# Conditioning matmuls from raw fp32 weights in four 32-column tiles, with buffers of their own for the head

## The chip, the core and the metric

The kernel runs on one core of one Trainium2 chip. The core has five engines: PE (TensorE, matmuls), DVE (VectorE), ACT (ScalarE), POOL (GpSimd) and SP (SyncE, which here only issues DMAs). The metric is the time of one execution on the device in microseconds (us).

## What is computed

A transformer-like model of two blocks, all in fp32, 256 tokens of `x` and 256 of `ctx`, width 1024. The first block has two layers; each is steered by nine conditioning vectors per stream, made from one vector `c` (for `x`) or `c_ctx` (for `ctx`). The change is about these vectors:

```python
mx = jnp.split(jax.nn.silu(c) @ ada_w[layer] + ada_b[layer], N_MOD, axis=-1)
mc = jnp.split((jax.nn.silu(c_ctx) @ ada_w[layer] + ada_b[layer])[None, :], N_MOD, axis=-1)
x = x + 0.5 * mx[2][:, None] * swiglu(modulate(rms_norm(x), mx[0], mx[1]), ffn1_w_gu[layer], ffn1_w_down[layer])
...
hx = modulate(rms_norm(x), mx[3], mx[4])
...
x = x + mx[5][:, None] * merge_mixers(...)
x = x + 0.5 * mx[8][:, None] * swiglu(modulate(rms_norm(x), mx[6], mx[7]), ffn2_w_gu[layer], ffn2_w_down[layer])
```

Here `modulate(h, shift, scale)` is `h * (1 + scale) + shift`. So 18 groups (two layers, nine vectors) are needed, each a product of two vectors of 1024 with a matrix of 1024x1024. The rest, feed-forward layers, a mixer of attention, pooling and a Fourier transform, and a second block with four other mixers, is not touched by the change except for the numbering of its weights.

## The kernel before

**Slots.** All weights come from one array `stream` of 816 slots of 128x1024 fp32 (512 KB each) in the order of use. SP loads slot n into `raw[n % 4]` (a ring of four). ACT makes the upper half, `whi` (fp32r, L1033); DVE the rest, `wlo = raw - whi` (L1491); both are rings of four too. PE waits for `w_ready` and multiplies in three fp32r matmuls (`mm3`, L419 to L421): upper times upper, upper times lower, lower times upper. A slot of `raw` is loaded again when its `wlo` is done (`w_ready`), a slot of `whi` and `wlo` is written again when PE is done with it (`slots_done`).

**The conditioning.** A group is eight slots (one for each 128 of the contraction). The vectors silu(c) and silu(c_ctx) are the stationary operand, as `cst4`: four columns (upper and lower of both), padded to 128. `ada` (L506 to L513) gives for each slot four fp32r matmuls with 512 columns into banks 4 and 5: two halves of the slot, each with `whi` and `wlo`. After eight slots ACT copies 4x1024 to `ada_row` (`ada_rows`, L1139), PE transposes it in eight pieces of 4x128 (`ada_cols`, L527), and DVE adds both parts and `ada_b` into `mod` (`ada_mod`, L1678 and L1681).

**Where the groups stand.** Two at the start (`ada_head`, 16 slots; before them nothing can be normalised, as `fix`, made from the scale of group 1, enters `norm_mod`). Five in `ffn1_up0`, five in `ffn2_up0`, four in `ffn1_up1`: there a loop handles 16 slots a pass, eight up-projection tiles (gate and up in turn, 24 matmuls with 512 columns each, the first two interleaved in `joint_tiles`) and eight conditioning slots between them, as `ADA_GROUP` says. Two more in `in0`, the first layer's mixer input: after each of tiles 1 to 8 two conditioning slots. So 14 groups are in loops, two in `in0`, two in the head.

**Order.** Everything is by hand: each engine has its own program, with waits on semaphores. In `ffn_up` ACT and DVE split the slots three or four ahead of PE and do a unit (silu of the gate, product with up, split into `hh` and `hl`) for each pair of tiles. In the head, ACT's squares of `X` for the first norm stand between the splits of slots 11 to 15, POOL adds them (L2094), PE sums (`norm_sums`, L438), ACT takes the root, PE spreads it; then DVE and ACT make `nh` and `nl` (`norm_mod`, L1566, and L1075, L1556), and the first `joint_tiles` follows them.

## Time and profile before

| | us |
|---|---|
| median of three runs | 3071.42 |
| lowest, highest | 3066.06, 3074.35 |
| span of the profiled execution | 3071.1 |
| PE busy | 2945.6 (96%) |
| DVE busy | 1690.4 (55%) |
| ACT busy | 1332.7 (43%) |
| POOL busy | 204.1 (7%) |

The profile shows one execution. An instruction's row has its start from the beginning of the span and its length; matmuls are pipelined, so their distance counts and not their length. A share of busy time is an average over stages: a loss is read from what an engine waited for in a stage. The granted clock is the share of TensorE's full clock (1.0 is 2.4 GHz, 0.5 is 1.2 GHz) that it was given.

### The profile page before, as it was taken

The numbers are of one execution on the slowest core, as the hardware profiler recorded it, in microseconds if no ns is written. First come the engines' busy times: TensorE is split into PE (matmuls) and PEld (weight loads), VectorE is DVE, ScalarE is ACT, GpSimd is POOL, SyncE is SP. The second block draws the span as 40 slices with busy tenths as digits, with TensorE's granted clock in tenths as the row PEclk, the third lists the DMA queues.
The fourth block names the chain that finished last, engine by engine and source line by source line (L and its number), as shares of the span: only waits on it lengthen the run. The fifth ranks groups of instructions, "written<-read, shape, count | busy, mean of one in ns | idle before, by whom it ended". The sixth has DMA issues, their size and how long they took to land. (4 is left out here: it accounts for less than half of the span.)

```text
span 3071.1 us, 48943 instructions
## 1 busy us (share of the span) xinstructions
PE 2945.6 (96%) x17866; PEld 2573.3 (84%) x17866; DVE 1690.4 (55%) x2279; ACT 1332.7 (43%) x1862; POOL 204.1 (7%) x224
## 2 busy tenths in 40 slices
PE   6999999999999999999988999899999999999998
PEld 5878887567787878888866998899999999998998
DVE  6444326646444244443265556976557476659864
ACT  5433325335343134332244445554545345545553
POOL 1000001200000000000020001300300000003100
PEclk7999999999999999999988999999999999999999
DMA  6445324113444225443222554355536556553453
GB/s 217 159 149 171 117 89 159 55 42 123 150 159 148 96 73 167 157 137 98 94 98 100 184 188 137 111 168 197 179 120 192 192 174 216 191 174 104 162 196 132
DMA packets 120488, 443.57 MB, mean 144 GB/s; under 512 B 13568, under 2 KB 14976, under 8 KB 119744
## 3 DMA queue, kind: packets, MB, share of 16 engines
q1 hardware_dynamic: 119376, 431.38, 42.6%
q0 software_dynamic: 1008, 10.75, 0.9%
q8 instruction: 71, 1.16, 0.2%
q14 instruction: 33, 0.27, 0.0%
HBM read 441.03 MB, written 1.05 MB: 144 GB/s over the span
## 5 line engine op out<-in xcount | busy, mean ns | idle before, releaser
L1491 DVE TENSOR_TENSOR wlo<-raw,whi 128x1024 fp32r<-128x1024 f32 x816 | 1001.0, 1240 | 922.4 <-ACT whi L1033 911.3
L1033 ACT ACTIVATE whi<-raw 128x1024 fp32r<-128x1024 f32 x816 | 848.8, 1054 | 942.7 <-PE ps L421 920.4
L419 PE MATMUL ps<-nh,whi 128*128 128x512 f32 (+1 forms) x1696 | 626.0, 369 | 20.1 <-DVE nl L1556 17.3
L420 PE MATMUL ps<-nl,whi 128*128 128x512 f32 (+1 forms) x1696 | 620.9, 366 | 0.0
L421 PE MATMUL ps<-nh,wlo 128*128 128x512 f32 (+1 forms) x1696 | 620.6, 366 | 0.0
L419 PE MATMUL ps<-bh,whi 128*128 128x256 f32 x1664 | 479.1, 288 | 10.8 <-DVE bl L1578 7.6
L420 PE MATMUL ps<-bl,whi 128*128 128x256 f32 x1664 | 468.8, 282 | 0.0
L421 PE MATMUL ps<-bh,wlo 128*128 128x256 f32 x1664 | 468.6, 282 | 0.0
L419 PEld LDWEIGHTS ps<-nh,whi 128*128 128x128 f32 x1696 | 323.0, 190 | 83.5 <-issue 19.3
L421 PEld LDWEIGHTS ps<-nh,wlo 128*128 128x128 f32 x1696 | 322.5, 190 | 56.1
L420 PEld LDWEIGHTS ps<-nl,whi 128*128 128x128 f32 x1696 | 323.0, 190 | 54.3 <-issue 0.2
L419 PEld LDWEIGHTS ps<-bh,whi 128*128 128x128 f32 x1664 | 314.8, 189 | 19.2 <-DVE bl L1578 13.0
L420 PEld LDWEIGHTS ps<-bl,whi 128*128 128x128 f32 x1664 | 315.1, 189 | 0.5
L421 PEld LDWEIGHTS ps<-bh,wlo 128*128 128x128 f32 x1664 | 315.0, 189 | 0.0
L419 PE MATMUL ps<-mh,whi 128*128 (+1 forms) x1024 | 287.7, 281 | 0.0
L420 PE MATMUL ps<-ml,whi 128*128 (+1 forms) x1024 | 287.7, 281 | 0.0
L421 PE MATMUL ps<-mh,wlo 128*128 (+1 forms) x1024 | 287.7, 281 | 0.0
L421 PE MATMUL ps<-hh,wlo 128*128 (+2 forms) x704 | 259.6, 369 | 0.0
L419 PE MATMUL ps<-hh,whi 128*128 (+2 forms) x704 | 257.9, 366 | 0.0
L420 PE MATMUL ps<-hl,whi 128*128 (+1 forms) x528 | 207.7, 393 | 0.0
L419 PEld LDWEIGHTS ps<-mh,whi 128*128 128x128 f32 x1024 | 192.9, 188 | 0.0
L420 PEld LDWEIGHTS ps<-ml,whi 128*128 128x128 f32 x1024 | 192.9, 188 | 0.0
(216 smaller groups left out, 3354.5 us busy)
## 6 DMA issues: line engine op xcount, KB each, us to landing
raw<-stream SPq DMA_DIRECT2D x816, 512.0 KB, 3.4
gates_w<-gate_in POOLq DMA_DIRECT2D x2, 3328.0 KB, 13.5
cst<-cst_in POOLq DMA_DIRECT2D x2, 1280.0 KB, 5.8
X<-x_in SPq DMA_DIRECT2D x1, 2048.0 KB, 11.7
out<-X SPq DMA_DIRECT2D x8, 128.0 KB, 2.0
fftw<-fftw_in POOLq DMA_DIRECT2D x2, 256.0 KB, 5.8
ws<-ws_in POOLq DMA_DIRECT2D x1, 512.0 KB, 4.4
poolw<-poolw_in POOLq DMA_DIRECT2D x2, 128.0 KB, 5.6
```

Of the source, the lines that this page charges most:

```text
L419: pe.matmul(dst, w1, rhs_hi, start=start, stop=False)
L420: pe.matmul(dst, w1, rhs_lo, start=False, stop=False)
L421: return pe.matmul(dst, w2, rhs_hi, start=False, stop=stop)
L1033: act.activation(whi[:, r, :], raw[:, r, :], ACT.Copy).then_inc(w_hi_ready, 1)
L1491: dve.tensor_tensor(wlo[:, r, :], raw[:, r, :], whi[:, r, :].bitcast(F32), ALU.subtract).then_inc(w_ready, 1)
```

## The change

Conditioning slots are not split any more. The two silu vectors lie in `csil`, fp32, padded to 32 columns. For a pair of slots PE issues four plain fp32 matmuls (`ada_streams`): each half of each slot goes to one quarter of bank 4's partitions, which is one 32-column tile of the array. One bank is used instead of two. ACT copies all 128 partitions of it (128x512) to `ada_row`; `ada_cols` multiplies four blocks of `ada_row` with `pick`, a 128x4 pattern of ones that adds even and odd slots; DVE adds `ada_b` in one instruction.

The slots are numbered anew: `AT` counts the split ones ("main") alone, `ORDER` is the order of loading, `SOURCE` the slot in `stream`, `PLACE` the place in the order. The ring `raw` still has four places, shared by both kinds: a place that held a main slot is free at its `w_ready`, one that held a conditioning slot at `ada_mm`, which PE raises after the pair. In a pass of the loop a pair stands behind tiles 2, 3, 4 and 5 (of 0 to 7).

The 16 slots of the head go to buffers of their own (`head`, in memory used later by the hidden layer), in eight DMAs of two slots; `X` is loaded first, and the squares are made at once. SP's loop is written out.

```diff
+ADA_AFTER = {2: 0, 3: 1, 4: 2, 5: 3}
...
+            def load(n):
+
+                if n >= RING:
+                    before, q = ORDER[n - RING]
+                    if before == "main":
+                        sp.wait_ge(w_ready, q + 1)
+                    else:
+                        sp.wait_ge(ada_mm, q // 2 + 1)
+                sp.dma_start(raw[:, n % RING, :], stream[SOURCE[n]]).then_inc(raw_loaded[n % RING], 16)
...
             sp.dma_start(cvec[:], cvec_in).then_inc(cond_loaded, 16)
...
             sp.dma_start(X[:], x_in).then_inc(x_loaded, 16)
...
+            for n in range(HEAD_PAIRS):
+                if n == 4:
+                    sp.dma_start(ident[:], ident_in).then_inc(vec_loaded, 16)
+                    sp.dma_start(ada_b[:], ada_b_in).then_inc(vec_loaded, 16)
+                    sp.dma_start(vec[:], vec_in).then_inc(vec_loaded, 16)
+                if n == HEAD_PAIRS - 1:
+                    load(0)
+                    load(1)
+                load_head(n)
+            for n in range(2, len(ORDER)):
+                load(n)
...
-            def ada(at, dyn, kt):
-
-                weights(at, dyn)
-                for b in range(2):
-                    for w in (whi, wlo):
-                        last = pe.matmul(bank(4 + b), cst4[:, 4 * kt:4 * kt + P],
-                                         w[:, at % RING, b * 512:(b + 1) * 512],
-                                         start=(kt == 0 and w is whi), stop=(kt == KD - 1 and w is wlo))
-                last.then_inc(slots_done, 1)
+            def ada_streams(pair, even, odd):
+
+                for kt, src in ((2 * pair, even), (2 * pair + 1, odd)):
+                    for half in range(2):
+                        q = 32 * (2 * (kt % 2) + half)
+                        last = pe.matmul(ps[q:q + 32, 4, :], csil[:, kt, :], src[:, half * 512:(half + 1) * 512],
+                                         start=(pair == 0), stop=(pair == KD // 2 - 1))
+                last.then_inc(ada_mm, 1)
...
-                for m in range(KD):
-                    last = pe.transpose(ps[:, 6, 4 * m:4 * m + 4], ada_row[:, m * P:(m + 1) * P],
-                                        ident[0:4, 0:4])
+                for m in range(4):
+                    last = pe.matmul(ps[:, 6, 4 * m:4 * m + 4], ada_row[:, m * P:(m + 1) * P], pick[:],
+                                     start=True, stop=True)
...
                         for u in range(4):
-                            for q in range(4):
-                                split(at + 4 * u + q + 3, i * 16)
+                            split(at + 2 * u + 3, i * 8, i * 64)
                             if u == 3:
-                                done(at + 14, i * 16)
                                 ada_rows(c["ada"], i)
-                            unit(at + ADA_GROUP.index(("gate", u)), i * 16, c["unit"] + u, i * 4, w, False, u, i * 4)
...
+                            unit(at + 2 * u, i * 8, c["unit"] + u, i * 4, w, False, u, i * 4,
+                                 between=lambda: split(at + 2 * u + 4, i * 8, i * 64))
...
                 for i in range(IN_TILES):
-                    split_to(in_slot(l, i) + 3)
+                    split_to(in_slot(l, i) + (3 if l else 1))
```

PE in a pass of the loop of `ffn1_up0`, behind the tile at whose end the first pair of conditioning slots stands. In each row `ps` is the output, the first name the moving operand, the second the stationary one; `whi` and `wlo` are the split slots. Before:

```order
L421 MATMUL ps<-nh_63,wlo_52 128x512
L412 REGISTER_ALU
L512 MATMUL ps<-whi_51,cst4_65 128x512
L512 MATMUL ps<-wlo_52,cst4_65 128x512
L512 MATMUL ps<-whi_51,cst4_65 128x512
L512 MATMUL ps<-wlo_52,cst4_65 128x512
L412 REGISTER_ALU
L512 MATMUL ps<-whi_51,cst4_65 128x512
L512 MATMUL ps<-wlo_52,cst4_65 128x512
L512 MATMUL ps<-whi_51,cst4_65 128x512
L512 MATMUL ps<-wlo_52,cst4_65 128x512
```

And after:

```order
L494 MATMUL ps<-nh_64,wlo_52 128x512
L585 MATMUL ps<-raw_50,csil_66 32x512 x4
L621 REGISTER_ALU
L485 REGISTER_ALU
L492 MATMUL ps<-nh_64,whi_51 128x512
```

Eight matmuls on split slots have become four on `raw`, each with an output of 32 partitions.

SP from its start; the arrow points from what is loaded. Before:

```order
L385 DMA cvec<-cvec_in 128x16
L386 DMA ada_b<-ada_b_in 128x288
L388 DMA raw<-stream 128x1024 x4
L389 DMA X<-x_in 128x4096
L390 DMA vec<-vec_in 128x280
L391 DMA ident<-ident_in 128x128
```

And after:

```order
L458 DMA cvec<-cvec_in 128x16
L459 DMA X<-x_in 128x4096
L455 DMA head<-stream 128x2x1024 x4
L462 DMA ident<-ident_in 128x128
L463 DMA ada_b<-ada_b_in 128x288
L464 DMA vec<-vec_in 128x280
L455 DMA head<-stream 128x2x1024 x3
L452 DMA raw<-stream 128x1024 x2
L455 DMA head<-stream 128x2x1024
L452 DMA raw<-stream 128x1024 x798
```

`X` has moved in front of all weights, and no load of the head waits for a split.

DVE from its start up to the first `norm_mod` instruction; `wlo` is a split, `mod` the conditioning's sum, `tok_inv` the norm's. Before:

```order
L1491 TENSOR_TENSOR wlo<-raw,whi 128x1024 x11
L1678 TENSOR_TENSOR mod<-ps,ada_b 128x16
L1681 TENSOR_TENSOR mod<-mod,ps 128x16
L1491 TENSOR_TENSOR wlo<-raw,whi 128x1024 x6
L1521 TENSOR_TENSOR sqsum<-sqsum,tmpb 128x512
L1523 TENSOR_TENSOR sqsum<-sqsum,tmpb 128x512
L1491 TENSOR_TENSOR wlo<-raw,whi 128x1024
L1511 TENSOR_SCALAR tok_inv<-ps 128x4
L1512 RECIPROCAL tok_inv<-tok_inv 128x4
L1491 TENSOR_TENSOR wlo<-raw,whi 128x1024
```

And after:

```order
L1929 TENSOR_TENSOR pick<-ident 128x4
L1584 TENSOR_TENSOR sqsum<-sqsum,tmpb 128x512
L1586 TENSOR_TENSOR sqsum<-sqsum,tmpb 128x512
L1740 TENSOR_TENSOR mod<-ps,ada_b 128x16
L1574 TENSOR_SCALAR tok_inv<-ps 128x4
L1575 RECIPROCAL tok_inv<-tok_inv 128x4
L1554 TENSOR_TENSOR wlo<-raw,whi 128x1024 x2
L1740 TENSOR_TENSOR mod<-ps,ada_b 128x16
L1554 TENSOR_TENSOR wlo<-raw,whi 128x1024
L1665 TENSOR_SCALAR fix<-mod 128x16
```

Of 19 splits three are left in front of `fix`, one of them between the second sum into `mod` and `fix`.

## Rows read from the trace of the kernel before

**Rows 1.** The page: its span, and the clock in 40 slices, in tenths.

```profile
span 3071.1 us, 48943 instructions
...
PEclk7999999999999999999988999999999999999999
```

**Rows 2.** PE's waits: waiting line, releaser, us in total, times, longest.

```profile
PE ps L438 <- DVE sqsum L1523: 23.7, 8, 4.6
...
PE ps L512 <- DVE wlo L1491: 13.5, 4, 7.6
```

**Rows 3.** Busy time by stretch: head twice, one pass of the conditioned loop.

```profile
core 0: us, PE busy (x) PEld busy (x) DVE busy (x) ACT busy (x) POOL busy (x), PEclk, DMA share, GB/s
0.00:10.00 10.00, 2.05 (x4) 1.17 (x4) 2.44 (x3) 4.72 (x6) 0.58 (x6) 1.00 0.79 283
10.00:20.00 10.00, 5.47 (x13) 4.09 (x14) 4.27 (x5) 3.56 (x5) 0.00 (x0) 0.90 0.93 379
...
161.73:214.83 53.10, 53.10 (x234) 42.51 (x233) 24.57 (x26) 21.21 (x25) 0.00 (x0) 1.00 0.48 160
```

**Rows 4.** Timeline of PE in the loop: start, length, engine, line, operation.

```profile
155.81 0.40 PE L512 MATMUL ps<-whi,cst 128*128 128x512 f32 x1
...
156.75 0.40 PE L419 MATMUL ps<-nh,whi 128*128 128x512 f32 x1
...
162.12 0.40 PE L421 MATMUL ps<-nh,wlo 128*128 128x512 f32 x1
162.45 0.65 PE L527 MATMUL ps<-ident,ada_row 4*128 4x4 f32 x8
163.03 0.50 PE L419 MATMUL ps<-nh,whi 128*128 128x512 f32 x1
163.37 0.40 PE L420 MATMUL ps<-nl,whi 128*128 128x512 f32 x1
...
215.55 0.59 PE L527 MATMUL ps<-ident,ada_row 4*128 4x4 f32 x7
```

**Rows 5.** Timeline of PE in the first mixer: plain fp32 matmuls, two records each.

```profile
530.59 4.17 PE L767 MATMUL ps<-cst,kqs 128*128 128x2 f32 x32
...
578.88 3.70 PE L828 MATMUL ps<-yt,fftw 128*128 128x512 f32 x8 [0.52 <-DVE yt L1828]
...
585.95 1.99 PE L682 MATMUL ps<-kq 64*128 64x512 f32 x8 [1.66 <-DVE nl L1835]
```

**Rows 6.** The line that issues slot loads, 83.5 to 86 us.

```profile
L396 SPq DMA_DIRECT2D raw<-stream x2: 333/333/333, 84.0 to 85.1; - x2
...
DMA to landing us min/median/max: 3.4/3.8/4.2
```

**Rows 7.** Timeline of the head's first loads and splits.

```profile
1.75 1.85 SPq L388 DMA_DIRECT2D raw<-stream  x4
...
5.12 1.06 ACT L1033 ACTIVATE whi<-raw 128x1024 fp32r<-128x1024 f32 x1 [0.99 <-DMA raw<-stream]
...
7.58 0.77 PE L512 MATMUL ps<-whi,cst 128*128 128x512 f32 x1 [7.58 <-DVE wlo L1491]
...
7.87 1.06 ACT L1033 ACTIVATE whi<-raw 128x1024 fp32r<-128x1024 f32 x1 [1.69 <-DMA raw<-stream]
...
9.11 1.06 ACT L1033 ACTIVATE whi<-raw 128x1024 fp32r<-128x1024 f32 x1 [0.18 <-DMA raw<-stream]
```

**Rows 8.** Timeline of the head's end: sums, conditioning, first norm.

```profile
34.47 4.06 POOL L2094 TENSOR_TENSOR sqsum<-sqsum,tmpb 128x512 f32<-128x512 f32 x2 [0.92 <-ACT tmpb L1055]
...
45.44 1.87 PE L438 MATMUL ps<-ones,sqsum 128*128 128x1 f32 x8 [4.57 <-DVE sqsum L1523]
...
49.26 1.01 ACT L1139 ACTIVATE ada_row<-ps 4x1024 f32<-4x1024 f32 x1 [0.36 <-PE ps L512]
...
52.00 1.66 DVE L1566 SCALAR_TENSOR_TENSOR tmpb<-X,fix,ps 128x256 f32<-128x256 f32 x4
```

**Rows 9.** Busy time of line L512 alone, 489 to 560 us (in0).

```profile
489.00:560.00 71.00, 18.35 (x64) 12.97 (x64) 0.95 0.54 182
```

More of the change, by code:

```diff
@@ L81, with _main, _ada @@
              ("gate", 2), ("up", 2), ("ada", 4), ("ada", 5), ("ada", 6), ("gate", 3), ("ada", 7), ("up", 3)]
+HEAD_ADA = 2
+HEAD_PAIRS = HEAD_ADA * KD // 2
+GROUPS = {"ffn1_up0": 5, "ffn2_up0": 5, "ffn1_up1": 4}
+ADA_AFTER = {2: 0, 3: 1, 4: 2, 5: 3}
+ORDER = []
+SOURCE = []
+AT = {}
+_mains = 0
+_a = HEAD_ADA * KD
+def _main(slot):
+    global _mains
+    ORDER.append(("main", _mains))
+    SOURCE.append(slot)
+    _mains += 1
+def _ada(slots):
+    global _a
+    for slot in slots:
+        ORDER.append(("ada", _a))
+        SOURCE.append(slot)
+        _a += 1
+for _name, _k in PLAN[1:]:
+    AT[_name] = _mains
+    _at = START[_name]
+    if _name in GROUPS:
+        for _g in range(GROUPS[_name]):
+            for _m in range(8):
+                _main(_at + ADA_GROUP.index((("gate", "up")[_m % 2], _m // 2)))
+                if _m in ADA_AFTER:
+                    _ada([_at + ADA_GROUP.index(("ada", 2 * ADA_AFTER[_m] + _n)) for _n in range(2)])
+            _at += 16
+        for _m in range(_at, START[_name] + _k):
+            _main(_m)
+    elif _name == "in0":
+        for _m in range(IN_TILES):
+            _main(_at + max(_m, min(3 * _m - 2, _m + 16)))
+            if 1 <= _m <= KD:
+                _ada([_at + 3 * _m - 1, _at + 3 * _m])
+    else:
+        for _m in range(_at, _at + _k):
+            _main(_m)
+N_MAIN = _mains
+assert _a == DEPTH * N_MOD * KD and len(ORDER) + HEAD_ADA * KD == N_SLOTS
+PLACE = {what: n for n, what in enumerate(ORDER)}
 GATE_K = {m: [k for k in range(max(0, m - 1), min(NR, m + 2))
@@ L163, in build @@
         hidden_s_end = mixer + 8 * NF * S
+        place[0] = mixer
+        head = sb("head", [P, HEAD_ADA * KD, SLOT])
+        assert place[0] <= mixer + 8 * NF * T
         place[0] = mixer
@@ L240, in build @@
         raw_loaded = [sem(f"raw_loaded{r}") for r in range(RING)]
+        head_loaded = [sem(f"head_loaded{n}") for n in range(HEAD_PAIRS)]
+        ada_mm = sem("ada_mm")
+        pick_ready = sem("pick_ready")
         w_hi_ready = sem("w_hi_ready")
@@ L1243, in mixer1 @@
                     if l == 0 and i in (5, 9):
-                        done(in_slot(l, i) - 1)
                         ada_rows(c["ada"], 0)
```

265 lines of the change are left out of this document (122 added, 143 removed).

## The prediction

> **What bounds the kernel now.** Start at the page's heading, then the clock row: the span is 3071.1 us and TensorE's granted clock is 0.8 to 1.0 outside the first slice [rows 1]. Then the waits of PE: the longest group is the norm sums, 23.7 us in eight waits; the conditioning matmuls (L512) waited 13.5 us, in four, all in the head [rows 2]. So between the head and the norms PE itself is the bound. The split work of ScalarE and VectorE is beside it: in one pass of the conditioned up-loop, 53.10 us, PE is busy for 53.10, DVE 24.57, ACT 21.21 and DMA moves 160 GB/s [rows 3]. In the head it is the other way round: in 10 to 20 us the DMAs move 379 GB/s and PE is half idle [rows 3].
>
> The profiled execution took 3071.1 us, 0.3 below the median of the runs shown (3071.42). I sum against 3071.1 and take the small difference as nothing. About 0.3%, 9 us, is what a measurement of this kernel can tell from no change: faster is below 3062, slower is above 3081.
>
> **What a conditioning pair costs before.** One slot is four fp32r matmuls of 512 columns: 155.81 to 156.75, 0.93 us with a start about 0.232 after the last [rows 4]. A pair is 1.86; four pairs of a group are 7.43. The eight transposes behind a group cost 162.12 to 163.37 less two ordinary steps of 0.235, 0.78 us. A pass is 215.55 - 162.45 = 53.10 us, so one of its eight 24-matmul tiles is (53.10 - 7.43 - 0.78) / 8 = 5.61 us [rows 4].
>
> **What a pair costs after (X).** It is four plain fp32 matmuls, 512 columns each, one in each quarter of the array's columns. Plain fp32 shows two records a matmul: eight records of L828 start every 0.43 us, 3.70 with the tail [rows 5]. One after the other, four would stream for 3.43 us. But eight records of L682, with 64 rows of contraction so that two fit in the array, end after 1.99 us instead of 3.6, so tiles of the array do overlap, and each keeps its own 0.43 a record [rows 5]. No row has 32-column tiles together; I take the nearest, L682, and let all four overlap: 2 x 0.43, plus 3 x 0.04 for staggered starts (estimated from the 1.99: 0.16 tail and four steps of 0.43 leave 0.1). Changing the array's tiling costs: into the 4-row transposes the step is 0.33 instead of 0.23, out of them 0.34 [rows 4], about 0.1 on the step before and 0.1 on the first step after, so 0.4 for both ways. X = 0.86 + 0.12 + 0.39 = 1.37 us. The bounds are 1.25 (no stagger) and 3.43 + 0.39 = 3.82 (no overlap). The Trainium skill, "TensorE: Matmul & The Clock Gate", Part 3, gives 2.38 times for three column tiles; spread over four (an estimate by that page) the pair would be 3.43/3.17 + 0.39 = 1.47 and the sum some 3 us higher. No run here shows it.
>
> **The ring is the catch.** Before, a slot of raw came free when its split was done. Now a conditioning slot is free only when PE has read it, and there are still four. Write the load order of a group: M0 M1 M2 A A M3 A A M4 A A M5 A A M6 M7. M4 takes the place of the second A of pair 0, so its load is issued only at the end of pair 0, behind the load of another A released by the same event. It is needed after tile 3 and pair 1, that is 5.61 + 1.37 = 6.98 us later. M5 stands so to pair 1, M6 to pair 2. What the load needs (L): two loads issued 1.13 us apart landed 3.4 and 4.2 after their issues, the second 5.3 after the first [rows 6]; in the head, four issued within 1.85 us landed 3.4, 6.1 and 7.4 after the first [rows 7]; when queued densely the step is 1.25, so 4.6 is the least. I take 5.2, near the steady row. From landing to PE (5.12 to 7.58) is 2.46: the 1.06 us split copy, the 1.23 us subtraction and handovers [rows 7]. L = 0.05 + 5.2 + 2.46 = 7.7, between 7.1 and 8.6. PE stalls 7.7 - 6.98 = 0.7; the stall delays the next need but not the next load, so M5 just arrives and M6 stalls again: two stalls in four tiles. M0 and M1 of the next group have two tiles more and are covered by them. Cost of a group: 2X + 2(L - 5.61) = 2.74 + 4.18 = 6.92 against 7.43. The end of a group is now four fp32 matmuls with ada_row as weights, eight records of narrow output; 32 of L767 took 4.17 with a cold end, 0.112 each while warm: 0.9 instead of 0.78 [rows 5]. **Fourteen groups: 14 x (-0.51 + 0.12) = -5.5 us.**
>
> **The mixer's input stage (in0).** Eight pairs, one tile between each. Its 64 matmuls keep PE busy for 18.35 us (two spells at low clock) [rows 9], about 18.1 by starts. After: 8 x 1.37 = 10.96, stalls by the same rule at M3, M5, M7, M9: 4 x 0.72 = 2.9. And one new wait: ScalarE copies ada_row at tile 5 behind the split of M6, whose load begins at the end of pair 4: 0.05 + 5.2 + 1.06 + 0.6 (square root) + 0.6 (copy) = 7.6, while tile 5 ends 0.7 + 5.6 = 6.3 after it; PE waits 1.3. Queued behind that wait are pair 5 and tile 6, which then need no stall of their own. 15.2 against 18.1: **-3 us**.
>
> **The head.** Before, norm_mod starts at 52.00, since fix needs the scale of group 1. Its chain: splits of 16 slots through the ring, squares of X on ScalarE between them, norm sums at 45.44, ada_row at 49.26 behind the last conditioning matmul, then 52.00 [rows 8]. After, the 16 slots go unsplit to eight buffers of their own and X is loaded first. Then the DMAs bound it. Before the last pair lands: X 2.10 MB, heads 8.39, two raw slots 1.05, small ones 0.36, 11.9 MB; 2.8 MB in the first 10 us at 283 GB/s, the other 9.1 at 379 [rows 3]: 34.0 us. X lands near 8 us; its squares feed five POOL additions of 2.0 each [rows 8], over by about 20, and sums and root by 29, all under the loads. Last pair at the low clock: twice 0.98 plus changes, 2.1, to 36.1; ada_row with handover 0.8, 36.9 (half the columns of the 1.01 before [rows 8]); eight narrow records 1.9 as for L438 [rows 8], 38.8; the addition 0.2; then VectorE's split of slot 2 stands in front of fix, 1.2; fix 0.2: norm_mod at 40.4. **-11.6 us**, between -8 (379 GB/s not held) and -14 (warm PE). The first joint tiles still have the slow start behind norm_mod.
>
> The 144 splits that go (1.06 on ACT, 1.23 on DVE) lie beside PE: nothing. Their loads stay. SP's loop is now a list of 798 loads; an issue takes 0.4 to 0.5 us against 5.6 per tile: nothing. POOL has only a shorter memset.
>
> **Sum:** 3071.1 - 5.5 - 3 - 11.6 = **3051 us**. With L 7.1 the groups give -22 and in0 -5.5: 3031. With L 8.1: 3065.
>
> **Rivals.**
> 1. *The ring takes it all* (L 8.2 to 8.6, as in the head's landings [rows 7]). Then a group costs up to 8.7, +1.4 with the columns, 14 times +20; in0 0; head -11.6: up to 3079, about 3070 in the middle. For it: three loads are released together. Against: the steady landing [rows 6].
> 2. *Passes in order.* If the records start in program order, the second record of a tile waits for its first, and only neighbours overlap: five steps of 0.43, X = 2.54. No ring stall then (5.61 + 2.54 = 8.15). Groups 14 x (10.16 - 7.43 + 0.12) = +40, in0 +4, head -11: 3104. If instead streaming is limited to what an fp32r stream reads now (512 columns in 0.23), 8 x 0.23 + 0.39 = 2.2: 3082. For it: four tiles read four different streams from the same partitions, which L682 with its halves doesn't. Against: the 1.99 of L682 is four steps; in program order, with two matmuls of one half before two of the other, it would be seven [rows 5]. The same page of the Trainium skill, Part 3, states that matmuls start and end strictly in program order; by that, X would be the 2.54 and the time 3104. By that rule, the trace disagrees for L682.
> 3. *No overlap*, the slower side: X = 3.82. It decides as soon as X passes about 2.1, where groups and in0 eat up the head. Groups 14 x (15.28 - 7.43 + 0.12) = +112, in0 +14, and the head becomes PE-bound, eight pairs of 3.8 from 10.5 on plus sums, columns and a slow start, norm_mod at about 50: 3195. For it: no row with column tiles side by side. Against: L682.
> 4. *The loads do not run as the order says* (X late, or a wait of SP blocks those behind it) and the head gives only 5: about 3058, inside the forecast's range.
>
> **Chances.** Forecast (X 1.3 to 1.5, 3031 to 3062, rival 4 within it) 0.59; rival 1 0.13; rival 2 0.15; rival 3 0.11; others 0.02. Faster by over 0.3%: 0.58. Same: 0.14 (most of rival 1, the edge of rival 2). Slower: 0.28. The range takes the forecast, rival 1 and rival 2, leaving out rival 3 and the lowest end: 3032 to 3104. The forecast's own range is 3031 to 3065.
>
> **What would show it.** X: the records of the new matmul in a group; right if the next tile starts 1.3 to 1.5 after the first, wrong at 2.2, 2.5 or 3.8. The ring: PE waiting for the subtraction of M4 and M6, 0.3 to 1.2 each, none for M5; wrong if there is none or at all three. A pass of the loop is 52.7 instead of 53.1. in0: one wait for ada_row near tile 5. The head: the first norm_mod at 40 instead of 52; wrong above 44. The likeliest failure is X, since it is taken from a tiling in rows, not in columns; next L, taken from landings at other spacings.

## The result, and the profile of the changed kernel

The changed kernel takes 3028.58 us (median, 3022.03 to 3028.98) against 3072.87 for the kernel before in the same measurement: a ratio of 0.985, with a 95% interval of 0.984 to 0.987. It is faster by 44 us. Forecast were 3051 us and a range of 3032 to 3104, so the direction was right and the gain was twice the forecast one, just outside the range.

First the page of the changed kernel, heading and busy times, and PE's waits (line that waits, releaser, us in total, times, longest):

```profile
span 3020.3 us, 45778 instructions
...
PE 2887.0 (96%) x17866; PEld 2486.2 (82%) x17866; DVE 1503.4 (50%) x2117; ACT 1182.9 (39%) x1717; POOL 197.4 (7%) x224
```

```profile
PE ps L511 <- DVE sqsum L1586: 19.2, 7, 3.6
PE ps L492 <- DVE nl L1619: 18.1, 6, 4.4
PE ps L492 <- DVE wlo L1554: 16.2, 30, 1.3
PE ps L585 <- DMA head<-stream: 15.7, 5, 12.1
```

PE is still the bound. Against [rows 2] the norm sums wait once less and 4.5 us less; the 13.5 us for the first splits have become 15.7 us of waiting for head loads; and a wait is new: 30 times, 16.2 us in all, for the subtraction of an ordinary slot (`wlo`, the lower half that DVE makes).

**The loop.** Two conditioning pairs of one pass (L585, eight records each), the split of the slot that the tile behind the second one needs (L1109 on ACT, L1554 on DVE), and the columns at its end (L606); start, length, engine, line. They answer to [rows 4]:

```profile
160.10 0.39 PE L494 MATMUL ps<-nh,wlo 128*128 128x512 f32 x1
160.42 1.06 PE L585 MATMUL ps<-raw,csil 128*32 128x512 f32 x8
161.41 0.50 PE L492 MATMUL ps<-nh,whi 128*128 128x512 f32 x1
161.75 0.39 PE L493 MATMUL ps<-nl,whi 128*128 128x512 f32 x1
...
166.28 1.06 ACT L1109 ACTIVATE whi<-raw 128x1024 fp32r<-128x1024 f32 x1 [11.19 <-DMA raw<-stream]
...
167.08 1.07 PE L585 MATMUL ps<-raw,csil 128*32 128x512 f32 x8
...
167.37 1.23 DVE L1554 TENSOR_TENSOR wlo<-raw,whi 128x1024 fp32r<-128x1024 f32 x1 [11.43 <-ACT whi L1109]
...
168.65 0.50 PE L492 MATMUL ps<-nh,whi 128*128 128x512 f32 x1 [0.50 <-DVE wlo L1554]
168.99 0.39 PE L493 MATMUL ps<-nl,whi 128*128 128x512 f32 x1
...
193.49 0.95 PE L606 MATMUL ps<-pick,ada_row 128*128 128x4 f32 x8
194.30 0.48 PE L492 MATMUL ps<-nh,whi 128*128 128x512 f32 x1
```

From the start of the pair to the next tile are 161.41 - 160.42 = 0.99 us. The step into it is 0.32 instead of an ordinary 0.227, the first step behind it 0.34: with both differences a pair costs X = 0.99 + 0.09 + 0.11 = 1.20 us; before it cost 1.86. In this pass the pairs behind tiles 2 and 4 have no stall; the pair behind tile 3 is followed by one: 1.57 to the next tile, against 0.99. The stalled tile starts 168.65 - 161.41 = 7.24 us after the end of the pair that freed its slot: that is the time of the ring, L. Of it, 166.28 - 161.41 = 4.87 us pass until ACT has the landed load, and 168.65 - 166.28 = 2.37 from there to PE. The columns cost 194.30 - 193.49 = 0.81, and with the steps around them 0.90.

The same pass as a whole, in the order of [rows 3] (us, then busy times; PEclk, DMA share, GB/s), is 50.39 us where it was 53.10:

```profile
143.10:193.49 50.39, 49.47 (x233) 37.26 (x232) 14.52 (x17) 13.06 (x17) 0.00 (x0) 1.00 0.45 166
```

**The head**, its end as a timeline (answers to [rows 8]), and its DMA from 10 to 20 us (answers to [rows 3]):

```profile
31.69 3.11 PE L585 MATMUL ps<-head,csil 128*32 128x512 f32 x16
...
34.93 0.60 ACT L1216 ACTIVATE ada_row<-ps 128x512 f32<-128x512 f32 x1 [2.90 <-PE ps L585]
...
35.58 1.05 PE L606 MATMUL ps<-pick,ada_row 128*128 128x4 f32 x8 [0.79 <-ACT ada_row L1216]
...
36.77 1.22 DVE L1554 TENSOR_TENSOR wlo<-raw,whi 128x1024 fp32r<-128x1024 f32 x1
37.90 0.17 DVE L1665 TENSOR_SCALAR fix<-mod 128x16 f32<-128x16 f32 x1
38.10 1.66 DVE L1629 SCALAR_TENSOR_TENSOR tmpb<-X,fix,ps 128x256 f32<-128x256 f32 x4
```

```profile
10.00:20.00 10.00, 6.04 (x28) 0.83 (x32) 0.00 (x0) 5.38 (x9) 6.33 (x5) 1.00 1.03 407
```

norm_mod starts at 38.10 instead of 52.00, with the split of a slot in front of `fix`, as the forecast had it.

**The ordinary matmuls.** This is what the forecast did not have at all. Groups of one line of an ordinary tile by shape (busy us, mean ns of one), first before, then after:

```profile
L420 PE MATMUL ps<-nl,whi 128*128 128x512 f32 x1216 | 484.9, 399 | 0.0
...
L420 PE MATMUL ps<-bl,whi 128*128 128x256 f32 x1664 | 468.8, 282 | 0.0
```

```profile
L493 PE MATMUL ps<-nl,whi 128*128 128x512 f32 x1216 | 478.1, 393 | 0.0
...
L493 PE MATMUL ps<-bl,whi 128*128 128x256 f32 x1664 | 473.6, 285 | 0.0
```

### The profile page after: what moved, and what is told of

It is laid out like the page before. It is cut to its first block and busy times, and to the rows that moved or that the text cites. A ratio compares the mean times of both kernels' runs of the same rounds, so it can differ in the third digit from the quotient of the medians.

```text
span 3020.3 us, 45778 instructions
## 1 busy us (share of the span) xinstructions
PE 2887.0 (96%) x17866; PEld 2486.2 (82%) x17866; DVE 1503.4 (50%) x2117; ACT 1182.9 (39%) x1717; POOL 197.4 (7%) x224
## 3 DMA queue, kind: packets, MB, share of 16 engines
HBM read 441.03 MB, written 1.05 MB: 146 GB/s over the span
## 5 line engine op out<-in xcount | busy, mean ns | idle before, releaser
L1554 DVE TENSOR_TENSOR wlo<-raw,whi 128x1024 fp32r<-128x1024 f32 x672 | 827.0, 1234 | 975.5 <-ACT whi L1109 973.1
L1109 ACT ACTIVATE whi<-raw 128x1024 fp32r<-128x1024 f32 x672 | 706.7, 1054 | 1020.1 <-PE ps L494 633.2
L492 PEld LDWEIGHTS ps<-bh,whi 128*128 128x128 f32 x1664 | 321.8, 193 | 17.7 <-DVE bl L1641 12.0
L493 PEld LDWEIGHTS ps<-bl,whi 128*128 128x128 f32 x1664 | 322.2, 194 | 0.5
L494 PEld LDWEIGHTS ps<-bh,wlo 128*128 128x128 f32 x1664 | 322.0, 193 | 0.0
## 6 DMA issues: line engine op xcount, KB each, us to landing
gates_w<-gate_in POOLq DMA_DIRECT2D x2, 3328.0 KB, 13.5
```

Of the source, the lines that this page charges most:

```text
L492: pe.matmul(dst, w1, rhs_hi, start=start, stop=False)
L493: pe.matmul(dst, w1, rhs_lo, start=False, stop=False)
L494: return pe.matmul(dst, w2, rhs_hi, start=False, stop=stop)
L1109: act.activation(whi[:, at % RING, :], raw[:, n % RING, :], ACT.Copy).then_inc(w_hi_ready, 1)
L1554: dve.tensor_tensor(wlo[:, r, :], raw[:, PLACE["main", at] % RING, :], whi[:, r, :].bitcast(F32), ALU.subtract).then_inc(w_ready, 1)
```

## Experiments

### Is it the place of the buffers? Padding, and no padding

The kernel before with nothing but 32 unused bytes a partition ahead of `nh`:

```diff
         ident = sb("ident", [P, P])
+        spare = sb("spare", [P, 8])
         sqsum = sb("sqsum", [P, T])
```

> The kernel before, with one unused buffer of 32 bytes per partition ahead of sqsum; no instruction changes, but nh, nl, bh, bl and all that lies behind them move by 32 bytes, as pick moves them in the changed kernel. Address theory (a matmul's step depends on where its data lie): the step of the 512-column matmuls of the up tiles falls from 0.234 to 0.227 us, that of the 256-column matmuls of the second block rises from 0.117 to 0.120; a pass of the conditioned loop takes 51.8 instead of 53.1; in all 3648 x -0.0065 = -24 us and about +20 us, so 3068 against 3072, no clear difference in time. Rival (less work of ACT and DVE on the same memory, or PE's other program, made the step shorter): steps stay at 0.234 and 0.117, a pass at 53.1, time at 3072.

The changed kernel with `pick` behind the other buffers, so that `nh` and `bh` lie where they lay before (`hh` does not move by this; it stays where the change has put it):

```diff
-        pick = sb("pick", [P, 4])
         sqsum = sb("sqsum", [P, T])
...
         fix = sb("fix", [P, DEPTH * 5, KD, 2])
+        pick = sb("pick", [P, 4])
```

> The changed kernel with pick laid behind fix, so that nh, nl, bh and bl lie where they lay before the change; nothing else differs. Address theory: steps go back to 0.234 and 0.117; the up tiles cost 24 us more, the second block and the narrow layer 20 us less, and the ring stalls of the loops shrink by some 4 us as the tiles get longer: about 3029, as the changed kernel's 3028.6. Rival (traffic or program): steps stay at 0.227 and 0.120, time 3028.6.

Measured: the padded kernel before 3061.43 us (0.997 of 3071.09, interval 0.9955 to 0.9987), the changed kernel without the shift 3028.86 (0.985, 0.984 to 0.987). The two shapes in the padded kernel, by line as above:

```profile
L421 PE MATMUL ps<-nl,whi 128*128 128x512 f32 x1216 | 477.4, 393 | 0.0
...
L421 PE MATMUL ps<-bl,whi 128*128 128x256 f32 x1664 | 472.0, 284 | 0.0
```

The steps follow the place: 0.227 and 0.120 in the padded kernel before, 0.234 and 0.117 in the changed kernel without the shift. What that brings differs: 10 us in the kernel before (some 4 were expected), nothing measurable in the changed one (3028.58 and 3028.86). A pass shows a part of why. Before and with padding, then without and with the shift after the change:

```profile
158.73:210.77 52.04, 52.04 (x233) 42.47 (x233) 24.56 (x26) 21.21 (x25) 0.00 (x0) 1.00 0.49 163
```

```profile
145.44:196.88 51.44, 50.64 (x233) 37.28 (x232) 14.54 (x17) 13.00 (x17) 0.00 (x0) 1.00 0.46 163
196.88:247.93 51.05, 50.68 (x234) 37.28 (x233) 14.60 (x17) 12.99 (x17) 0.00 (x0) 1.00 0.46 165
```

In the kernel before, faster tiles take 53.10 - 52.04 = 1.06 us off a pass. In the changed one they take off 51.2 - 50.4 = 0.8: a tile that is over sooner waits longer for its slot (waits for `wlo` 16.2 us with the shift, 13.0 without it). And the second block, with 256 columns, loses: 1186.7 us before, 1188.6 in the changed kernel without the shift, 1200.4 with it. So with `nh` and `bh` left where they were, the change is worth 42 us by itself. The shift gives with one hand and takes with the other; that the two cancel in the changed kernel is chance. (`hh` is not at its old place in this comparison, but its steps are on average the same to 0.1 ns with 512 columns and 2 ns shorter with 256, about 1 us in all.)

### Do the four tiles run at once?

All matmuls of a pair in one quarter of the array instead of four (the four streams of a pair are then summed, so the conditioning rows are others than the reference's):

```diff
-                        q = 32 * (2 * (kt % 2) + half)
+                        q = 32 * pair
                         last = pe.matmul(ps[q:q + 32, 4, :], csil[:, kt, :], src[:, half * 512:(half + 1) * 512],
-                                         start=(pair == 0), stop=(pair == KD // 2 - 1))
+                                         start=(kt % 2 == 0 and half == 0), stop=(kt % 2 == 1 and half == 1))
```

> The changed kernel, but all four fp32 matmuls of a pair go to one quarter of the array's columns (quarter 0 for pair 0, 1 for pair 1, and so on), so none can overlap; the four streams of a pair land on each other, so the conditioning vectors are not the reference's. Number, shape and operands of the matmuls are the same. Theory (the pair is cheap because its four column tiles run at the same time): a pair takes 8 x 0.43 plus 0.3 for the changes, 3.8 instead of 1.2; a loop pass 10.4 less 1.0 of ring stalls more, 59.7 instead of 50.3; 14 passes +131, in0 +18, head +12: about 3190. Rival (a matmul with 32 stationary columns is cheap by itself): a pair stays at 1.2, 3029.

Measured: 3166.62 us, ratio 1.030 (1.028 to 1.032). A pair:

```profile
132.59 3.62 PE L585 MATMUL ps<-raw,csil 128*32 128x512 f32 x8
136.15 0.50 PE L492 MATMUL ps<-nh,whi 128*128 128x512 f32 x1
```

3.55 us instead of 0.99: eight records 0.43 apart, one after the other, and 0.52 from the last to the next tile. Overlap in the four quarters saves 2.56 us a pair, and without it the change loses (rival 3 of the forecast put this case at 3195). The kernel lost 138 us. A pass takes 59.51 us, 9.1 more than 50.39: four times 2.56 less the stalls, which are gone (no wait for `wlo` is left). Fourteen passes are 128 us; the head ends only 4 us later, since its waits for loads take in the longer pairs, and in0 is 8 us longer. My expectation of 3190 had left these covers out.

### How far does the place reach?

The second block's buffers alone 32 bytes further, on the changed kernel:

```diff
-        place[0] = common
+        place[0] = common + 32
         bh = sb("bh", [P, KD, S], F32R)
```

> The changed kernel with the buffers of the second block alone moved by another 32 bytes (bh, bl and what follows); the first block stays. Address theory: the step of the second block's 256-column matmuls goes back from 0.120 to 0.117, the first block keeps 0.227 at 512 columns: about -17 us, 3011. Rival: no step changes, 3029.

Measured: 3006.44 us, ratio 0.979 (0.978 to 0.981). The second block's steps are 0.116 to 0.117 again, and 20 us are gained on the changed kernel.

Then the step by itself: behind the changed kernel's last work, with the other engines idle, strings of 21 matmuls as in a tile, at growing offsets into a live buffer that starts where `bh` does modulo 256 bytes:

```diff
+            mov_hi = oh[:].rearrange("p k n -> p (k n)")
+            mov_lo = ol[:].rearrange("p k n -> p (k n)")
+            def column(off, off_lo, cols):
+                for kt in range(KD - 1):
...
+                    pe.matmul(dst, w1, mov_hi[:, a:a + cols], start=(kt == 0), stop=False)
+                    pe.matmul(dst, w1, mov_lo[:, b:b + cols], start=False, stop=False)
+                    pe.matmul(dst, w2, mov_hi[:, a:a + cols], start=False, stop=(kt == KD - 2))
```

> The changed kernel, all of it, and behind its last step on TensorE a string of matmul triplets as in a tile (hi by hi, lo by hi, hi by lo weights) from the same live buffers: 21 matmuls of 512 columns and 21 of 256 for each of the offsets 0, 32, 64, 96, 128, 160, 192, 224 bytes, then 16 and 48 bytes, then 0 and 32 again, then with the two moving operands 32 bytes apart. Theory (the step of a matmul follows the place of its moving operand modulo 64 bytes, and nothing else): at 0, 64, 128 and 192 a 512-column step of 0.227 us and a 256-column one of 0.120; at 32, 96, 160 and 224 0.234 and 0.117; the mixed ones between. Rival (the step comes from what the other engines do to the memory at the time, the place only shifts that): with the other engines idle all offsets show one and the same step for each width. The columns are about 120 us behind the end of the ordinary work, so the time is about 3160 and says nothing else.

Neither theory held: with idle engines the step still depends on the place, but not modulo 64. Nor is it the operand's own place alone: with the lower operand (`mov_lo`) 32 bytes from the upper one, which stayed at the fast place, a step of 512 columns took 0.2329 us, not something between 0.2267 and 0.2335, and one of 256 columns 0.1170, less than at either place. The strings were repeated on `bh` and `bl`, on `oh` and `ol`, each with `wlo` and with a slot of `whi` as the third matmul's weights:

> The changed kernel and behind it, with the other engines idle, strings of 21 triplet matmuls at 512 and at 256 columns, at offsets 0, 32, 64, 96, 128 and 192 bytes: first with bh and bl as moving operands and wlo as the third matmul's weights, as the kernel has them, then with whi's next slot in wlo's place, then both again with oh and ol. Theory (place modulo 256 bytes alone): every set of four shows at 256 columns 0.120, 0.118, 0.113, 0.120, 0.120, 0.113. Rival (the place of the weights against the moving operand counts too): the first string, laid out as the second block is, shows 0.118 at 64 bytes as in the kernel with the second block 64 bytes on, and the string with whi's next slot 0.113. Rival two (the other engines' traffic made the 0.118 there): all show 0.113 at 64. The strings take about 210 us, so the time is about 3240.

The first strings of that run (stretch, length, PE busy and matmuls; 512 and 256 columns in turn, offsets 0 and 32 bytes; the last column but two is the granted clock):

```profile
3055.17:3059.93 4.76, 4.76 (x23) 3.94 (x22) 0.00 (x0) 0.00 (x0) 0.00 (x0) 1.00 0.00 0
3059.93:3062.44 2.51, 2.51 (x23) 2.51 (x21) 0.00 (x0) 0.00 (x0) 0.00 (x0) 1.00 0.00 0
3062.44:3067.34 4.90, 4.90 (x23) 3.94 (x22) 0.00 (x0) 0.00 (x0) 0.00 (x0) 1.00 0.00 0
3067.34:3069.82 2.48, 2.48 (x23) 2.48 (x21) 0.00 (x0) 0.00 (x0) 0.00 (x0) 1.00 0.00 0
```

Each stretch holds the starts of 21 matmuls, so 4.76 us is a step of 0.2267 and 4.90 one of 0.2333 (0.2335 with the starts to the nanosecond). The whole, by the place modulo 256 bytes; 32 and 96 are from the first run of strings. The places take the first free byte of the memory as 128 modulo 256, which no run prints; the distances between them are the kernel's own:

| place | 128 | 160 | 192 | 224 | 0 | 32 | 64 | 96 |
|---|---|---|---|---|---|---|---|---|
| step, 512 columns | 0.2267 | 0.2335 | 0.2297 | 0.2339 | 0.2328 | 0.2341 | 0.2333 | 0.2329 |
| step, 256 columns | 0.1196 | 0.1179 | 0.1133 | 0.1198 | 0.1198 | 0.1186 | 0.1136 | 0.1180 |

All four sets show these numbers within 0.001, so neither the buffer nor the weights' slot matters. The table also fits most of the working kernels (averages): `nh` at 96 before (0.2333, and 0.1183 with 256 columns) and 128 after (0.2274, 0.1200); `hh` at 64 after (0.2333, 0.1134); `hh` at 0 in the padded kernel (0.2333, 0.1187). One row does not fit: in the changed kernel without the shift `hh` lies at 64 as well, but its 256-column steps take 0.1178 us. So in a whole kernel something beside this place counts too.

The first run of strings had already given most of these numbers, and `hh` at 128 and the second block at 192 were forecast from it alone; the second block at 64 was forecast together with the second run of strings.

`hh` and the mixer's buffers 64 bytes further, to 128:

```diff
-        mixer = place[0]
+        mixer = place[0] + 64
+        place[0] = mixer
```

> The changed kernel with hh, hl and the mixer's buffers 64 bytes further on, which puts hh where nh lies modulo 256 bytes. Theory (place over 256 bytes): the 1965 steps of 512 columns that read hh and hl fall from 0.2335 to 0.227, 13 us, the 143 of 256 columns rise from 0.1135 to 0.120, 1 us; the two down stages end 12 us earlier, 3015 to 3019. Rival (hh's step has another cause, its place does nothing): 3028.5.

Measured: 3012.24 us, ratio 0.982 (0.980 to 0.985). The steps of `hh` are 0.227 and 0.120, as foretold. The gain on the changed kernel is 14 us if each is set against its own measurement of the kernel before, and 16 straight; 13 were forecast for the fast steps and 1 lost on the others. The line of `hl`, after and here:

```profile
L493 PE MATMUL ps<-hl,whi 128*128 x384 | 151.3, 394 | 0.0
```

```profile
L494 PE MATMUL ps<-hl,whi 128*128 x384 | 149.4, 389 | 0.0
```

The second block 64 and 192 bytes further (`common + 64`, `common + 192`), to places 192 and 64:

> The changed kernel with the buffers of the second block alone (bh and what follows) 64 bytes further on. The string of idle-engine matmuls behind the kernel gave 256-column steps of 0.1197 us at offset 0, 0.1178 at 32, 0.1133 at 64 and 0.1199 at 96 and 128, against theory one (modulo 64 bytes), which had 0 and 64 alike. Theory now (the step follows the place over at least 256 bytes, in the kernel as in the string): the second block's 8883 steps fall from 0.120 to 0.113, 57 us less in its stretch, 2966 to 2976. Rival (modulo 64 bytes after all, the string's 64 was an accident of its order): 3028.5. Rival two (beside working engines the gain shrinks): a step of 0.116 to 0.118, 2993 to 3011.

> The changed kernel with the second block's buffers 192 bytes further on, at 64 modulo 256, where hh has its 0.113 in the working kernel. Theory (modulo 256, and 192 of 256 was spoilt by something that 64 of 256 is free of): 256-column steps of 0.113 to 0.114 in the second block, 50 to 57 us less, 2972 to 2980. Rival (what is fast for hh is slow for bh, since more than the place modulo 256 counts): 0.117 to 0.120, 3005 to 3030.

Measured: 3006.96 us (0.981, 0.978 to 0.984) and 2994.18 us (0.975, 0.971 to 0.979). Here the table fails in part. At 192 all second-block steps are 0.117 to 0.118, not 0.113, and the 57 us that were forecast came to 22. At 64 the `oh` and `ol` steps are 0.113 to 0.114 as foretold, but those of `bh` and `mh` 0.116 to 0.118. So in the second block the fast places are only partly fast. Since the strings with idle engines used the same buffers and the same `wlo`, what the other engines do at the time is the likeliest reason, but no run isolates it; the strings also wrote to one PSUM bank only, where tiles alternate, which was not tried either.

### What the ring and ScalarE take

The pairs further apart, on the changed kernel:

```diff
-ADA_AFTER = {2: 0, 3: 1, 4: 2, 5: 3}
+ADA_AFTER = {1: 0, 3: 1, 5: 2, 6: 3}
```

> The changed kernel with the four conditioning pairs behind tiles 1, 3, 5 and 6 of a pass instead of 2, 3, 4 and 5. Theory (a ring slot comes round about 7.2 us after the pair that freed it, longer than one tile and one pair, so two pairs running one tile apart leave a stall of 0.5 us at every second tile): with a plain tile between the pairs the stalls at the conditioning pairs go, one of up to 0.9 us can stay at tile 7 or in the next pass, TensorE's waits for wlo fall from 16 us to 5 to 9, the pass from 50.4 to 49.8 to 50.2, and the time to 3020 to 3024. Rival (the stall is of the four loads together, by their bytes, wherever they lie): waits stay near 16 us, pass 50.4, time 3028.5.

With this table the split of one slot behind each set of passes reads another slot of `raw`, so its values are not the reference's; the work is the same. Measured: 3020.4 us, ratio 0.983 (0.980 to 0.985). A pass and the wait:

```profile
143.78:193.93 50.15, 49.71 (x234) 37.17 (x233) 14.76 (x17) 12.99 (x17) 0.00 (x0) 1.00 0.45 167
```

```profile
PE ps L492 <- DVE wlo L1554: 8.9, 17, 1.5
```

The pairs with a plain tile ahead of them (behind tiles 3 and 5) show no stall any more, only the pair behind tile 6 does: 17 waits of 30 and 8.9 us of 16.2 are left. The stall belongs to two pairs one tile apart, not to the bytes. Against its own kernel before it is 50 us faster, the changed kernel 44; the intervals overlap, so the waits show this gain and the times only that nothing is lost.

ScalarE's copy of the conditioning rows ahead of its splits in the mixer:

```diff
+                    if l == 0 and i in (5, 9):
+                        ada_rows(c["ada"], 0)
+                        c["ada"] += 1
```

> The changed kernel with ScalarE, in the first layer's token mixer, copying the conditioning rows out of PSUM ahead of the splits it does at tiles 5 and 9 instead of behind them. Theory (the 2.8 us that TensorE waits for ada_row at 493.6 is ScalarE doing its split, which waits for a weight load, ahead of the copy): that wait falls to 0 to 0.5 us, the two low-clock stretches at 495 to 498 and 505 to 512 may go with it, 3 to 8 us less in the profile of the layer's in-projection, 3021 to 3026. Rival (the copy waits for the pair on TensorE itself): the wait stays and the time at 3028.5.

Measured: 3020.95 us, ratio 0.984 (0.9825 to 0.986). First the place in the changed kernel, then here:

```profile
490.54 0.39 PE L494 MATMUL ps<-nh,wlo 128*128 128x512 f32 x1
493.61 1.06 PE L606 MATMUL ps<-pick,ada_row 128*128 128x4 f32 x8 [2.68 <-ACT ada_row L1216]
494.60 1.82 PE L585 MATMUL ps<-raw,csil 128*32 128x512 f32 x8
```

```profile
490.57 0.39 PE L494 MATMUL ps<-nh,wlo 128*128 128x512 f32 x1
490.80 0.95 PE L606 MATMUL ps<-pick,ada_row 128*128 128x4 f32 x8
491.68 1.06 PE L585 MATMUL ps<-raw,csil 128*32 128x512 f32 x8
```

The wait of 2.7 us is gone, so ScalarE's order made it. Of two stretches at half the clock behind it (494.8 to 498.2 and 505.0 to 511.8 us) one of 3.4 us is left; the stage between the norm sums at 442.9 and those at 668 takes 225.1 us instead of 230.6.

The first two ordinary loads behind the last head load instead of ahead of it:

```diff
             for n in range(HEAD_PAIRS):
...
-                if n == HEAD_PAIRS - 1:
-                    load(0)
-                    load(1)
                 load_head(n)
-            for n in range(2, len(ORDER)):
+            for n in range(len(ORDER)):
```

> The changed kernel with the first two 512 KB loads of the ordinary weights behind the last of the eight head loads instead of ahead of it. Theory (the head is bound by the bytes ahead of the last head load, 1 MB of which go behind it): the last head load lands 2.5 to 3 us earlier, near 31.3, norm_mod comes at 35.3 instead of 38.1 and the first ordinary matmul at 38.5 to 39; the kernel gains 2 to 2.8 us, about 3026. Rival (the head is bound by the chain that starts at the norm sums or by ScalarE, not by the bytes): norm_mod stays within 0.5 us of 38.1 and the time at 3028.5. Second rival: the ordinary weights become late instead and the first ordinary matmul waits for them until 41 or later: 3028.5 to 3030.

Measured: 3026.91 us, ratio 0.985 (0.983 to 0.987), which is the changed kernel's. The last head load, in the changed kernel and then here, with its time to landing:

```profile
L455 SPq DMA_DIRECT2D head<-stream x1: 433/433/433, 17.1 to 17.1; - x1
...
DMA to landing us min/median/max: 16.4/16.4/16.4
```

```profile
L455 SPq DMA_DIRECT2D head<-stream x1: 1089/1089/1089, 15.0 to 15.0; - x1
...
DMA to landing us min/median/max: 15.4/15.4/15.4
```

And the end of the head here:

```profile
30.14 1.12 PE L515 MATMUL ps<-ident,tok_rstd 128*128 128x128 f32 x4
...
32.34 0.12 PEld L582 LDWEIGHTS ps<-head,csil 128*32 128x32 f32 x4 [0.31 <-issue]
...
34.00 0.58 ACT L1213 ACTIVATE ada_row<-ps 128x512 f32<-128x512 f32 x1
...
37.14 1.66 DVE L1626 SCALAR_TENSOR_TENSOR tmpb<-X,fix,ps 128x256 f32<-128x256 f32 x4
```

The bytes did what the theory said: the last head load landed at 17.1 + 16.4 = 33.5 us before and at 15.0 + 15.4 = 30.4 here, 3.1 us earlier (31.3 was forecast). The head loads land in the order of issue, 2.56 us apart where they follow each other. But `norm_mod` comes at 37.14, only 1.0 us earlier, and half of that is not the edit's: in this run, as in the run without the shift, whose `norm_mod` is at 37.53, the first head pair comes 0.5 us earlier, which leaves 0.4. When the last load has landed, PE still has the matmuls that spread the norm (30.14) and the pair before the last one to do, and reaches the last pair only at 32.34; the granted clock was 0.50 from 27 to 31 us. ScalarE, in a split since 33.03, copies `ada_row` only at 34.00. So the first rival was near the truth: without these bytes the chain behind the norm sums and ScalarE bound the head.

### What is the change worth at equal places, and how good does it get?

The kernel before with `nh` at 128, `hh` at 128 and the second block at 192, then the changed kernel with the same places:

```diff
+        spare = sb("spare", [P, 8])
...
-        mixer = place[0]
+        mixer = place[0] + 128
+        place[0] = mixer
...
-        place[0] = common
+        place[0] = common + 64
```

> The kernel before with its buffers where the combined kernel has them modulo 256 bytes: nh 32 bytes on, hh 128 further, the second block 64 on from nh. Its steps should be 0.227 for nh and hh at 512 columns, 0.113 in the second block. Against the kernel before: 21 us for nh, 12 for hh, 33 for the second block (0.1175 to 0.1135), 3 lost on nh at 256 columns: about 3007. Theory: at equal places the change of the conditioning matmuls is worth what it was between the changed kernel with the buffers where they were before and the kernel before, 42 us. Rival (the change's worth shrinks when tiles are faster, since a ring slot comes round no sooner and its stalls grow): 5 to 10 us less.

> The changed kernel with the buffers where the kernel before with moved buffers has them modulo 256 bytes (second block and hh each 64 bytes on). The parts measured singly, 21.6 and 16.3 us, add to 2990.7 if they are independent. Against the kernel before with the same places (3039.9) that makes the change worth 49 us. Theory (worth at equal places 42 us, less 5 to 10 where tiles are faster): 3000 to 3008. Rival (the parts add): 2988 to 2994.

Measured: 3039.85 us (0.991, 0.988 to 0.993) and 2998.95 us (0.977, 0.9745 to 0.980). The kernel before was expected at 3007 and missed it by 33 us: its second block shows the 0.118 of place 192, not 0.1135, which is 38 us on 8900 steps. At three sets of places the change is worth 42 us (unshifted), 35 (both shifted by 32 bytes: 44.3 less 9.7) and 39 (these two: 70.3 less 31.1, each against its own kernel before). The intervals are several us wide, so the three do not differ clearly; only in the last set does `hh` too lie at one place in both kernels. The parts do not add quite: 16 and 22 us singly, 26 to 30 together.

Two combinations. The first has the places of the pair above, the rows' copy moved, the loads behind the head, and the pairs behind tiles 2, 4, 5 and 6. The second has `hh` 64 bytes on, the second block 32, and the rows' copy:

> All together on the changed kernel: the second block 64 bytes on, hh 64 bytes on, the conditioning pairs behind tiles 2, 4, 5 and 6, ScalarE's copy of the rows ahead of its splits, the two ordinary loads behind the head. If the parts add: 57 for the second block, 12 for hh, 4 for the pairs, 3 to 7 for the copy, 0.5 to 1 for the head, together 77 to 81 from 3028.5: 2947 to 2953. If the pairs need a plain tile on both sides as in the kernel with 1, 3, 5 and 6, the waits for wlo stay at 16 us and the time is 4 longer.

> The changed kernel with hh 64 bytes on, the second block 32 bytes on and ScalarE's copy of the rows ahead of its splits; pairs and head as in the changed kernel. If the parts add (16.3, 22.1 and 7.6 us singly): 2982.5, between 2978 and 2987, 8 below the combination with moved pairs, whose waits for ada_row at tile 7 (12 times 0.4 us) took what its shorter waits for wlo gave. Rival (the combination's 2990.5 was all that these places give, the pairs cost nothing): 2988 to 2993.

Measured: 2990.53 us (0.975, 0.973 to 0.978) and 2991.35 us (0.975, 0.972 to 0.977): the same, and 37 us below the changed kernel. Neither reached what its parts promised. In the first, the moved pairs traded one wait for another, as PE's waits show:

```profile
PE ps L490 <- DVE wlo L1552: 9.8, 17, 2.3
...
PE ps L490 <- ACT ada_row L1214: 4.6, 12, 0.6
```

The last pair now ends so late in the pass that PE, where it asks for `ada_row` ahead of the last three matmuls of tile 7, finds it not yet copied, 12 times. In the second the waits for `wlo` grew to 19.7 us.

## Why the forecast was off, step by step

The measure is the changed kernel with `nh` and `bh` where they were before, since the forecast assumed them there. It stands 40.4 us below the kernel before in the profiled executions (3030.7 against 3071.1), against 20 forecast. By stages that is 14.5 for the head, 26 for the groups in loops and 1.4 for the mixer's input, less 1.9 in the second block. **What failed is the cost of a group in the loops: the time of the ring, L, and the price of a pair, X, were both put too high.**

- **The head, forecast -11.6, measured -14.5 there and -13.9 in the changed kernel.** Right in its mechanism, and inside its bounds of -8 to -14 in the changed kernel. Landing of the last pair was forecast for 34.0; the last eight records start at 33.55. Shorter than forecast was the chain behind it: 38.10 - 33.55 = 4.6 us against the 6.4 summed. The eight narrow records took 1.05 instead of 1.9 (they were priced by norm sums at the low clock [rows 8]), and the last pair ran out in 1.4 instead of 2.1.
- **X, forecast 1.37, measured 1.20.** Records and stagger were right: 0.86 + 0.12 = 0.98 against 0.99. The mis-sized term is the change of tiling, 0.39 forecast, 0.20 measured: I priced 0.1 on each side of a pair for the way in and again for the way out, and it is paid once on each side. Rival 2, by which only neighbours overlap (2.54), fell, and so did rival 3 (3.82, and 3.75 where it was built). The Trainium skill, "TensorE: Matmul & The Clock Gate", Part 3, says that matmuls start and end strictly in program order; here the four instructions start in program order, the first records of all four tiles within 0.02 us and the second ones 0.45 later, so the rule holds and only my reading of it as a rule for single records did not. L682, which the forecast held against the rule, keeps it in the same way: the second records of its two tiles start 0.04 us apart, in order.
- **The ring, forecast two stalls of 0.7 a group.** In the changed kernel they are mostly 0.4 to 0.8 behind the second pair and 0.3 to 0.5 behind the fourth, and, but for one of 0.4, at most 0.1 behind the third: the pattern is as forecast, but L is 7.2 instead of 7.7, and most of the difference is the load (4.87 to ACT's start instead of 5.25 to its landing). With the slower tiles of the old places they are 0.6 to 1.0 a group in all, 0.8 on average, instead of 1.4. The stalls and X are the failed terms: a group gains 1.9 us (51.2 against 53.1) instead of 0.4, fourteen times: **-26 instead of -5.5. That is as much as the whole miss of 20; the other errors nearly cancel.** Two small errors in the same direction, 0.17 on X, four times, and 0.3 on each stall, were multiplied by 14. The forecast's low case (L at 7.1, 3031) was the right one, but the stated range began at 3032 and left it out.
- **Columns, forecast 0.90 a group, measured 0.90.** Right.
- **in0, forecast -3.** With the old places 232.6 us against 234.0 between the norm sums around it: -1.4. In the changed kernel two of the four stalls are there, of 0.9 and 1.1 us. The wait for `ada_row` was foreseen at its place, but at 1.3 us; it is 2.7, and behind it come two spells at a granted clock of 0.50, of 3.4 and 6.8 us, in which two more pairs take 1.8 and 1.9 us.
- **The splits that go, SP's issues: nothing.** Right: DVE is at 50% of the span and the loop's issues never hold PE.
- **What had no step at all: the ordinary matmuls.** 3600 steps of 512 columns went down by 6 ns on average and 10,300 of 256 up by 1.6, some 21 and 17 us. It nets nothing measurable in the changed kernel and so isn't the cause of the miss; but each half is about as large as the whole forecast gain, and I had not asked what 16 bytes ahead of every matmul operand do. That the halves cancel is luck.

So the reason for the gain was right, the head and cheaper pairs, and its split was wrong: I put most of it in the head, and two thirds lie in the fourteen groups.

## What to carry to other kernels

A term that stands in a loop deserves bounds that are multiplied by its count before the range is written down: 0.3 us on a stall is 8 us here. When a change adds or drops any buffer, ask which operands move, and look at the step of untouched matmuls first; moving buffers by 32 to 192 bytes was worth between nothing and 31 us on this kernel without touching an instruction. And when a ring of four takes direct readers, keep a plain tile between two of them, unless the last reader's result is needed at once.

## What the runs showed of the hardware

- The step of an fp32r matmul depends on where its moving operand begins: 0.2267 to 0.2341 us with 512 columns, 0.1133 to 0.1198 with 256, over the places modulo 256 bytes tried, with all other engines idle and at full granted clock. The best place for one width is not the best for the other. The distance to the neighbour's operand counts too (0.2329 and 0.1170 with 32 bytes between them). The Trainium skill, "SBUF — State Buffer", "Who interferes with whom", has only the port shared by VectorE and GpSimd as a point of contention. The strings agree as far as they go, since the effect needs no second engine; the `bh` steps of 0.118 in the kernel against 0.1133 in the string, at one place, stay unexplained, and so does `hh` with 0.1178 and 0.1134 at one place in two kernels.
- Four fp32 matmuls with 128x32 weights in the four column quarters start 7 ns apart and take 0.99 us together, against 3.55 one after the other: a factor of 3.6. The Trainium skill, "TensorE: Matmul & The Clock Gate", Part 3, has 2.38 for three; no run here has three.
- Queued loads landed in the order of issue, 1 MB each 2.56 us (410 GB/s): with 1 MB less ahead of it the last of eight landed 3.1 us earlier, 0.5 of them from the start of the run. Its user gained 0.4 us, since PE was not ready.
- Four plain fp32 matmuls with four columns each, weights of 128x128, eight records in all, hold PE for 0.81 us up to the next tile's start in the loop.
